# Delta rule of a four-mixer block: setup by pairs, projection steps inside the block products, bias rows written during the first jobs

## What is computed

```python
qkv = causal_conv_silu(proj[..., :A_CONV_CH], conv_w)      # 4 taps; then q, k are l2-normalised
a_mat = where(strict, einsum("bhncd,bhnsd->bhncs", k_beta, k) * decay, 0.0)
rhs = concatenate([v * beta[..., None], k_beta * exp(g)[..., None]], axis=-1)
sol = triangular_solve(a_mat + eye(CHUNK), rhs, left_side=True, lower=True, unit_diagonal=True)
qk_intra = where(tril, einsum("bhncd,bhnsd->bhncs", q, k) * decay, 0.0)
...
o = rms_norm(o, out_norm_g) * silu(z)
```

## Time and profile before

| what | us |
|---|---|
| median of 3 runs | 860.55 (859.98 to 864.71) |
| the profiled execution, its time | 857.89 |
| its span | 856.0, mean granted TensorE clock 0.986 |
| TensorE busy | 827.2 (97%) |
| VectorE, ScalarE, GpSimd busy | 602.2 (70%), 484.0 (57%), 42.0 (5%) |
| weight chunks, issue to landing | median 4.9 over 112 |

### The profile page before, as it was taken

How to read it: one execution, slowest core, us unless ns; L and a number is a source line. 1 busy time by engine, 2 the same in 40 slices (tenths; PEclk the granted TensorE clock), 3 DMA queues, 4 the chain that set the end, 5 groups by cost and what they waited for, 6 DMA issues and landing times. The chain is left out here.

```text
span 856.0 us, 18089 instructions
## 1 busy us (share of the span) xinstructions
PE 827.2 (97%) x7682; PEld 804.6 (94%) x7682; DVE 602.2 (70%) x1058; ACT 484.0 (57%) x746; POOL 42.0 (5%) x63
## 2 busy tenths in 40 slices
PE   6999879899999999999999999998999999999998
PEld 6899878898999999999999999998999999999998
DVE  5785667667887877596888885646678677565662
ACT  4765435445666564564454445345867767777731
POOL 4100000003600000000000000200000000000000
PEclk9999889899999999999999999999999999999999
DMA  7363371261876565447666564793456444434350
GB/s 279 111 242 129 51 188 58 102 221 57 237 236 245 199 244 198 148 154 281 217 234 238 210 244 147 198 289 123 179 197 224 166 156 178 163 119 177 133 188 25
DMA packets 26497, 153.84 MB, mean 180 GB/s; under 512 B 2848, under 2 KB 3376, under 8 KB 12080
## 3 DMA queue, kind: packets, MB, share of 16 engines
q1 hardware_dynamic: 24432, 146.37, 48.3%
q0 software_dynamic: 1984, 6.31, 4.2%
HBM read 150.04 MB, written 2.62 MB: 178 GB/s over the span
## 5 line engine op out<-in xcount | busy, mean ns | idle before, releaser
L1382 DVE TENSOR_TENSOR wlo<-raw,whi 128x1024 fp32r<-128x1024 f32 x224 | 266.1, 1225 | 128.8 <-ACT whi L980 128.8
L479 PE MATMUL ps<-hhi,whi 128*128 128x256 f32 x1024 | 297.3, 290 | 7.4 <-DVE hlo L1408 4.4
L980 ACT ACTIVATE whi<-raw 128x1024 fp32r<-128x1024 f32 x224 | 227.0, 1053 | 126.9 <-PE ps L479 87.5
L479 PE MATMUL ps<-hlo,whi 128*128 128x256 f32 x1024 | 292.6, 286 | 2.7 <-issue 2.7
L479 PE MATMUL ps<-hhi,wlo 128*128 128x256 f32 x1024 | 292.3, 285 | 1.0 <-issue 1.0
L479 PEld LDWEIGHTS ps<-hhi,whi 128*128 128x128 f32 x1024 | 198.7, 194 | 10.7 <-issue 6.4
L479 PEld LDWEIGHTS ps<-hlo,whi 128*128 128x128 f32 x1024 | 198.9, 194 | 3.4 <-issue 2.9
L479 PEld LDWEIGHTS ps<-hhi,wlo 128*128 128x128 f32 x1024 | 198.8, 194 | 1.2 <-issue 1.2
L479 PE MATMUL ps<-ohi,whi 128*128 128x256 f32 x448 | 128.8, 287 | 1.3 <-DVE olo L1427 1.2
L479 PE MATMUL ps<-ohi,wlo 128*128 128x256 f32 x448 | 126.7, 283 | 0.0
L479 PE MATMUL ps<-olo,whi 128*128 128x256 f32 x448 | 126.7, 283 | 0.0
(11 more groups left out here) (221 smaller groups left out, 967.7 us busy)
## 6 DMA issues: line engine op xcount, KB each, us to landing
raw<-weights SPq DMA_DIRECT2D x112, 1024.0 KB, 4.9
ada_ring<-ada SPq DMA_DIRECT2D x24, 1024.0 KB, 5.0
arena<-bias_rows_d POOLq DMA_DIRECT2D x4, 512.0 KB, 15.1
x<-x_t SPq DMA_DIRECT2D x2, 512.0 KB, 4.6
bias_rows_d<-early POOLq DMA_DIRECT2D x1, 1024.0 KB, 12.0
arena<-bias_rows_b POOLq DMA_DIRECT2D x4, 256.0 KB, 7.5
arena<-bias_rows_d POOLq DMA_DIRECT2D x4, 256.0 KB, 17.9
out_t<-x SPq DMA_DIRECT2D x4, 256.0 KB, 2.9
```

The lines of the kernel that those rows point to most:

```text
L479: return pe.matmul(o, l, r, start=start, stop=stop, skip_group_check=skip)
L980: act.activation(whi[:, unit % UNITS, :, :], raw[:, c % RAW, 4 * half:4 * half + 4, :], ACT.Copy).then_inc(hi_ok_sem, 1)
L1382: dve.tensor_tensor(wlo[:, unit % UNITS, :, :], raw[:, c % RAW, 4 * half:4 * half + 4, :], whi[:, unit % UNITS, :, :].bitcast(F32), ALU.su ...
```

## The change

Seven things change.

- `masked(p)` moves up behind the first product of each pair, and ScalarE takes state decay and decay pair by pair. `conv(8)` moves behind level 0's rows, and `low(9)` behind the first two pairs.
- `weave(n)` writes the next n steps, whatever job they belong to. The setup has 9, level 0 has 3, levels 1 to 5 have 9 each: one behind 6 and one behind 11 of the 16 matrices in the first and in the second products, two between the two, three at the end. Level 6 has 4 and 5. These are 66 steps; jobs 8 to 15 have 64.
- ScalarE makes a chunk's first half ahead of its level copies and the second behind them.
- `take_values` goes from VectorE to ScalarE.
- The modulation pairs of the delta rule are one instead of three. `ADA_AT` begins 14, 23, 25, and has 66 behind 62.
- Waits on `mod_ok` go up by one, because of that.
- The bias rows are written when `tap_ok` is 2, ScalarE's first tap of job 1.

```diff
-ADA_AT = [13, 14, 15, 25, 27, 29, 31, 33, 35, 42, 44, 46, 48, 50, 52, 54, 56, 58, 60, 62, 78, 82, 86, 90]
-ADA_EARLY = 3
+ADA_AT = [14, 23, 25, 27, 29, 31, 33, 35, 42, 44, 46, 48, 50, 52, 54, 56, 58, 60, 62, 66, 78, 82, 86, 90]
+ADA_EARLY = 1
...
+            def weave(n):
+
+                for _ in range(n):
+                    parts(8 + woven[0] // 8, woven[0] % 8, woven[0] % 8 + 1)
+                    woven[0] += 1
...
             products(0, 0)
+            masked(0)
             products(0, 1)
             products(1, 0)
-            parts(8, 0, 4)
+            masked(1)
+            weave(2)
             products(1, 1)
...
                 if last:
+                    ada(0, taken(slot_of_mod(0)))
+                    weave(4)
...
+                    weave(5)
                 else:
+                    weave(2)
                     pe.wait_ge(xc_ok_sem, lv)
                     pe.wait_ge(u32_ok_sem, lv)
-                    second_products(lv, 256 if lv < 5 else 0).then_inc(tp_ok_sem, 1)
-                parts(J, 4, 8)
+                    second_products(lv, 256 if lv < 5 else 0, (6, 11)).then_inc(tp_ok_sem, 1)
+                    weave(3)
...
+                if lv < LEVELS - 1:
+                    high(9 + lv, range(1))
+                    act.wait_ge(x_ok_sem, lv)
...
+                    high(9 + lv, range(1, 2))
+                    if lv >= 2:
+                        take_values(lv - 2)
...
             take_rows(0)
-            low(10)
+            conv(8)
             for lv in range(1, LEVELS - 1):
-                low(10 + lv)
+                if 2 <= lv <= 4:
+                    conv(7 + lv)
+                low(9 + lv)
```

More of the change, by code:

```diff
@@ L204, in two_blocks @@
                 turn_order.append(f"values{lv - 2}")
[L205 to L206 removed]
+            if lv == 6:
+                turn_order.append("mod0")
         turn_order += [f"sum{i}" for i in range(4)]
@@ L633, in _, with first_products @@
             products(0, 0)
+            masked(0)
             products(0, 1)
             products(1, 0)
-            parts(8, 0, 4)
+            masked(1)
+            weave(2)
             products(1, 1)
[L638 to L645, removed]
+            weave(2)
+            decay_rows(2)
+            products(2, 0)
             masked(2)
+            products(2, 1)
+            weave(2)
+            decay_rows(3)
+            products(3, 0)
             masked(3)
-            parts(9, 2, 4)
-            def first_products(lv, c0):
+            products(3, 1)
+            weave(3)
+            def first_products(lv, c0, between=()):
                 left = left_of(lv) if lv < 5 else lambda v: v
@@ L654, in first_products @@
                 for m16 in range(16):
+                    if m16 in between:
+                        weave(1)
                     o = slice(c0 + m16 * n, c0 + m16 * n + n)
@@ L658, in first_products, with second_products @@
                 return m
-            def second_products(lv, c0):
+            def second_products(lv, c0, between=()):
                 n = 16 if lv < 5 else 32
                 for m16 in range(16):
+                    if m16 in between:
+                        weave(1)
                     o, i = slice(c0 + m16 * n, c0 + m16 * n + n), slice(m16 * n, m16 * n + n)
@@ L1120, in _ @@
             state_decay(0)
+            decay(0)
             state_decay(1)
+            decay(1)
             high(9)
-            decay(0)
-            decay(1)
+            state_decay(2)
+            decay(2)
+            state_decay(3)
+            decay(3)
             first_tap(8)
-            state_decay(2)
-            state_decay(3)
-            decay(2)
-            decay(3)
-            high(10)
-            silu(8)
             def gate_z(J):
@@ L1372, in low @@
                     n = ADA_AT.index(c)
-                    if ADA_EARLY < n < 20:
+                    if ADA_EARLY < n < 20 and n != 8:
                         take_mod(n - 1)
@@ L1535, in pair_matrices @@
                 dve.tensor_tensor(qkd[:, b4, :], v2(bq, P), ee[p % 2], ALU.mult).then_inc(nt_ok_sem, 1)
-            low(9)
             pair_matrices(0)
             pair_matrices(1)
-            conv(8)
+            low(9)
             pair_matrices(2)
@@ L1584, in _ @@
                     take_halves()
-                if lv <= 3:
-                    conv(8 + lv)
-                if lv == 4:
-                    dve.wait_ge(sil_ok_sem, 1)
-                    pair_sums(0)
-                if lv == 5:
-                    mod_of_slot(0)
-                    pair_sums(1)
-            mod_of_slot(1)
-            pair_sums(2)
+            low(15)
+            dve.wait_ge(sil_ok_sem, 1)
+            pair_sums(0)
+            mod_of_slot(0)
             for g in range(4):
@@ L1770, in gains_of_c @@
             def gains_of_c():
-                for n in range(ADA_EARLY - 1):
-                    dve.wait_ge(slot(slot_of_mod(n))[1], slot(slot_of_mod(n))[2] + 1)
-                dve.wait_ge(mod_ok_sem, 6)
+                take_mod(7)
+                dve.wait_ge(slot(slot_of_mod(0))[1], slot(slot_of_mod(0))[2] + 1)
+                dve.wait_ge(mod_ok_sem, 7)
                 scaled_gain(0)
```

93 lines of the change are left out of this document (44 added, 49 removed).

## The result

The changed kernel takes 876.7 us (median of 4 runs, 873.23 to 877.87), beside 862.47 for the kernel before (4 runs, 859.98 to 864.71). The ratio is 1.0186, with a 95% interval of 1.0139 to 1.0233. It is slower, as forecast, but by 14.2 us and not 6.5, and it lies outside the range that was given. The profiled execution took 877.87 us with a span of 876.0, 20.0 more than the span of 856.0 before.

A forecast was written before the change was run, and what follows sets the result against it. TensorE, busy for 97% of the span, was taken to bound the kernel. Bias rows +7.4, delta rule -2.5 and modulation +1.6 made +6.5 us on 857.9, 864.4; with 2.7 for the median 867.1, range 855.5 to 873.

The forecast's parts named there:

- The bias rows, +7.4: Early jobs: the early bias writes delay job 6's weight chunk, 4.0 us lost waiting and 3.4 at the lower clock.
- Rival A: Early jobs: the queues share the engines, job 6 loses 0.5 us instead of 7.4; 860.2 us, 2 in 10.
- Rival C: Early jobs: bias rows also hold up job 5's chunk, 7.9 + 3.4 instead of 7.4; 871.0 us, 1.5 in 10.
- Setup, levels 0 and 1: Delta rule's start: setup 23.0 us plus 1.5 for low clock, level 0 4.4 us, level 1 12.0 us.
- Levels 2 to 4: Delta rule: remainder waits of 0.3, 1.1 and 2.8 us, another 0.3 for a half; 33.8 us, before 32.5.
- two steps inside 2.7: Delta rule levels: block products of one kind cost 1.26 us, with two projection steps inside 2.7 us.
- one stretch: Delta rule, after level 4 or 5: one stretch at 1.2 GHz, taking 1.5 us from the gain.
- Level 6 and the dead steps: Delta rule: level 6 takes 13.9 us against 13.2, two useless steps for job 16 cost 1.4 us.
- Modulation, +1.6: Moved modulation sums: the pair in job 23 delays job 24's weights by 1.6 us, the one behind chunk 66 costs 0.
- VectorE has room: 0: Behind chunk 66: a job is 11.5 us long, so VectorE takes the modulation sums there at no cost.
- -2.5: Delta rule: 6.2 us gained at full clock, 2.5 left after setup, one low-clock stretch and instruction code.
- rival B: Whole kernel: no wait in job 6 and the clock holds through the levels, -5.0 us; 855.5 us, 1.5 in 10.

The follow-up runs named there:

- kernel 2: Changed kernel with the sums of chunk 66's modulation pair taken to chunk 70 and their transfer issued later; ratio 1.0224 to the kernel before.
- kernel 3: Changed kernel with no step inside the block products, four between the two groups and five behind; ratio 1.0056 to the kernel before.
- kernel 5: Changed kernel with the modulation pair of chunk 66 at chunk 39 instead; ratio 1.0134 to the kernel before.
- kernel 6: Kernel before with only the bias rows written early, when job 1's first tap is done; ratio 0.9969.
- kernel 7: Changed kernel with steps outside the block products, the pair at chunk 39 and job 16's two steps left out; 857.6 us, ratio 0.9982 to the kernel before.
- kernel 4: Changed kernel with the bias rows written behind the pair matrices again, by the old wait; ratio 1.0219 to the kernel before.
- kernel 1: Kernel before with only the modulation sums' new places and the waits that go with them; ratio 1.0130.
- kernel 11: Kernel before with two of each level's eight steps inside the first products and two inside the second; ratio 1.0148.
- kernel 8: As kernel 7, with the bias rows written in six pieces of 0.25 MB, one behind each level's inverse; 854.9 us, ratio 0.9935 to the kernel before.
- kernel 9: Kernel before with only the bias rows written in six pieces, one behind each level; ratio 0.9944.
- kernel 12: As kernel 8, with the values taken by VectorE again; ratio 0.9940 to the kernel before.

## Why the prediction was wrong

**The bias rows, +7.4: right.** Measured 6.3 (25.76 - 19.48) in the profiled execution. With the same early write it is 6.2, 6.0 and 4.6 in kernels 2, 3 and 5, 3.3 in kernel 6 and 1.6 in kernel 7, so the cost varies with the kernel, and 7.4 is above all of them. The chunk landed at 61.1 instead of 62.4 and cost 4.2 us instead of 4.0; the clock after it was 0.57 for 8 us, by the stretch from 64 to 72. Rival A is out: between 42 and 44 GpSimd's queue moves alone. The Trainium skill (DMA: Bandwidth & Descriptors, "Queues, rings and completion order"), by which an engine goes round the queues packet by packet, doesn't describe the first write; it does fit the second, and the read back from 560 on (SP's queue 67%, GpSimd's 30% from 560 to 564). Rival C is out, since job 5's chunk took 4.7 us.

**Setup, levels 0 and 1: right.** 24.25, 4.43 and 12.23 us against 24.5, 4.4 and 12.0. The wait before masked(0) was 2.5, not 1.3. That the stalls on code go with the bias rows was in these numbers; kernels 6 and 4 show that it is worth 7 to 14 us in single executions, more than the trace of the kernel before let one see.

**Levels 2 to 4: the first step that failed is "two steps inside 2.7".** I added the price of two steps in a row to that of 128 products in one piece. A level by this sum is 9.7 us, and that is what it takes with the steps *outside* (9.62). With four inside it takes 11.08. By the rows of level 2 a group that is cut in three costs about 0.57 us (0.15 more for each of its two lone steps, 0.27 for the three pieces), so 1.1 of the 1.46 us; the rest these rows don't show. The Trainium skill (TensorEngine Tiling (Array Packing), "Key Properties") says that changing the tiling mode drains TensorE; the trace fits it, with 0.15 us more for a lone step, and the prediction had not weighed it. The waits went as told in place and partly in size: 2.1 in level 4 (forecast 2.8), none in levels 2 and 3, 1.0 and 1.1 in level 5 (1.5 and 1.1), and 1.3 at its last step (1.9), which the profile puts down to the remainder and not to the gate. Then the clock: 0.78 in level 3 and 0.88 in level 4 are 3.3 and 1.7 us, where 1.5 stood for one stretch. Level 3's came behind an issue wait of 1.5 us. Kernels 2 and 5 have the same level 3 in 11.2 us, so some 4 us of it belong to this execution and not to the change.

**Level 6 and the dead steps: right**, 13.92 against 13.9, and 1.45 us for the two steps against 1.4.

**Modulation, +1.6: the larger failed step is "VectorE has room: 0" for the sums behind chunk 66.** Job 24 lost 1.1 us, for 1.6. For chunk 66 the 0 was wrong twice. VectorE's busy time left room, but its order did not: the sums stand ahead of the addition to `x`, and TensorE waits 1.97 us. And they hold `ada_ring`, so that the next pair's transfer moves from chunk 65 (512 us) to chunk 69 (558 us), into the read back. I never looked at what the DMA engines do there, though the trace of the kernel before shows it: share 1.02 and chunks of 17.5 us. TensorE waits 3.89 us there, and the clock after the two waits costs 5.0; against that a wait of 1.1 us behind job 24 is gone, which the kernel before has. **9.1 us, the largest single miss**: kernels 1 and 5 show from both sides that it hangs on this place; the two halves of the cause are read from the rows.

Together: 1.1 at the start that no part of the change explains (the kernels here begin job 5 anywhere between 53.8 and 56.5), 6.3 for 7.4, 2.4 for -2.5, 1.1 and 9.1 for 1.6: 20.0 for 6.5. By the medians it is 14.2, because the profiled execution of the kernel before is one of its faster ones and that of the changed kernel is its slowest. Two slips in the prediction's sums matter little: the terms of levels 2 to 4 add up to 33.6 and not 33.8, and rival B has 1.2 where the modulation's term is 1.6.

## What to carry over

A moved computation also moves whatever waits for its buffer, here the next transfer: look at what stands behind it on its own engine, and at the DMA share where that transfer will be issued. By kernels 3 and 11, filler between small matmuls belongs between their groups, not inside them, and its steps should be no further ahead of their weights and banks than the other engines are. A long write on one queue can stall weights and instruction code alike; cut it in pieces before looking for a place where it fits.

## What the runs showed of the hardware

- A write of 1 MB with 16 rows repeated 32 times lands 12 us after its issue. For some 8 us of them (39 to 47 in the changed kernel) it has 96% of the engines at 100 GB/s, and no packet of another queue moves. The write of 0.5 MB with 8 rows behind it takes about half of the engines' time, and weight packets move beside it. The two stalls of 11.4 and 12.1 us on "issue" begin in the first write and end only late in the second. TensorE goes on some 2.3 us after its code packet has been carried (116.75 to 119.06). The Trainium skill (Runtime: NRT & Kernel Launch, "Instruction fetch mechanics") has code fetch mostly hidden; here it isn't.
- With pieces of 0.25 MB the longest issue waits are 1.4 and 1.3 us in kernel 8 (levels 2 and 4), but 2.1 and 2.5 in kernel 9 (levels 1 and 2) and 3.2 in kernel 12 (level 4). What is left of them with no bias write at all (1 to 2 us in kernel 6) wasn't taken further.
- Which of two equal stretches falls to the lower clock differs between executions and kernels: level 6 at 0.69 in kernel 7 and at 1.00 in kernel 8. What decides it stays open.
